# Two of four prefetched weight loads requested as 120 and 8 partitions

## The chip, the cores and the metric

The kernel runs on one core of one Trainium2 chip. The metric is the device time of one execution in microseconds; the time before is the median of 3 runs, 1379.53 us (1378.22 to 1382.62).

## The reference, cut to what matters

Two transformer blocks run one after the other over 256 tokens of width 1024. The first ends with a layer of single experts ("PEER"): from the normalized token a query is made with the weights w_pq, 1024 x 2048; scores against two sets of 128 sub-keys pick 16 of 16384 experts for each of 8 heads; each expert is one row of `expert_down` and one of `expert_up`.

```
def block(xb):
    qh = (xb @ w_pq).reshape(T, P_HEADS, 2, P_KEY_DIM)
    s1 = einsum('thd,nd->thn', qh[:, :, 0], sub_keys1)
    s2 = einsum('thd,nd->thn', qh[:, :, 1], sub_keys2)
    ...
    top_s, pos = lax.top_k(cand_s, P_TOPK)
    eidx = jnp.take_along_axis(cand_i, pos, axis=-1)
    g = jax.nn.softmax(top_s, axis=-1)
    u = expert_down[eidx]
    a = gelu(einsum('thkd,td->thk', u, xb))
    return einsum('thk,thkd->td', g * a, expert_up[eidx])
```

So 8 x 16 x 256 = 32768 rows of 2048 floats (down and up side by side, 8 KB) are fetched by index, 268 MB. The second block (gated linear attention, block attention, a feed-forward of 4096, a gate) is dense and follows.

## The kernel before, in words

All dense weights are cut into halves of 128 partitions x 2048 floats, 1 MB each, in the order of `HALVES`. SyncE (SP) requests one half at a time into a ring of three buffers (`ring`). ScalarE copies a half as the high part of a split product (line 1529) and VectorE subtracts to get the low part (line 2107); TensorE then multiplies three combinations of parts (`prod`, its matmuls on line 859). A request into the ring waits until the low part of the half that last held the buffer is made.

The query weights w_pq are eight halves, pq 0,0 to pq 3,1, numbered from `FIRST_PQ`. Four of them, numbers +1, +2, +6 and +7, don't go through the ring: `AHEAD` gives each a buffer of its own (`raw`, which shares memory with the split parts `hl`), so that they can be fetched before the expert rows. `ASKED_FOR` puts their requests after that of number +5, in the order +6, +7, +1, +2. Each waits on TensorE (line 757) until a half that used the memory has been multiplied (`LEFT`). Each has its semaphore, and ScalarE's split of the half waits for it (`ld`). Number +1 is split first, right after the half `FIRST_PQ`; numbers +2 to +7 are split between the expert rows, one per head.

The expert rows are 256 indirect gathers issued by GpSimd (line 823): gather i fetches one row of 8 KB for each of 128 tokens, 1 MB, into one of `NG` = 8 buffers `rows`. Gather i waits until TensorE is done with gather i - 8, and the first ones also for the indices. Gathers 0 to 7 and 8 to 15 need the first head's indices for the first 128 tokens, gather 16 those for the other 128. For each pair of gathers VectorE makes the dot products with the token (line 2615), ScalarE the gelu (line 1797) and a diagonal matrix of the coefficients (line 1804), and TensorE adds the rows, weighted by it, into PSUM (line 1242). The next load on SP, the first half of `gv` (lines 761 to 763), waits for gather 254.

Of the kernel before, what the change touches and what calls it, by code (L numbers as in the profile page):

```python
# [27 lines left out]
FIRST = {}  # L28
# [38 lines left out]
def program(nc, A, out):  # L67
    ctx = ExitStack()
    with ctx:
# [3 lines left out]
        def count(name, keys, by=1):  # L73
            return Count(ctx.enter_context(nc.semaphore(name)), keys, by)
# [148 lines left out]
        LAST_XO, FIRST_PQ = NUM["xo", 1, 1], NUM["pq", 0, 0]  # L223
# [23 lines left out]
        def loaded(n):  # L247

            if HALVES[n][0] == "ple":
                return PWB[:, :]  # L250
            if n in AHEAD:
                return AHEAD[n][:, :]
            return ring[:, RINGED.index(n) % RING, :]
# [22 lines left out]
        ld = {}  # L276
        for i in range(RING):
            ld.update(count(f"ring{i}", RINGED[i::RING], 16))
        ld[NUM["ple", 0, 0]] = at["wple"]
        for n in AHEAD:  # L280
            ld.update(count(f"ahead{n}", [n], 16))

        GV = NUM["gv", 0, 0]
        gv_first = landed("gv_first")
# [367 lines left out]
        n = NUM["xo", 0, 0]  # L652
# [20 lines left out]
        n = NUM["gv", 0, 0]  # L673
# [52 lines left out]
        for k in range(8):  # L726
            for h in range(2):
                n = NUM["dn", k, h]
# [16 lines left out]
        @block.sync  # L745
        def _(e):
            for tb in range(2):
                e.dma_start(X[:, tb, :], A["x"][tb * 128:tb * 128 + 128, :]).then_inc(at[f"x{tb}"][0], 16)
            for n in ASKED_FOR:
                name, k, h = HALVES[n]  # L750
                if (name, k, h) == ("xv", 0, 0):
                    e.dma_start(PWB[:, :], A["wple"]).then_inc(at["wple"][0], 16)
                    e.dma_start(pT[:, :, :], A["pT"]).then_inc(at["pT"][0], 16)
                if name == "ple":
                    continue
                if n in AHEAD:
                    e.wait_ge(*pe[USED[LEFT[n]]])
                elif RINGED.index(n) >= RING:
                    e.wait_ge(*lo[RINGED[RINGED.index(n) - RING]])
                if n == GV:  # L760
                    e.wait_ge(*gath[254])
                    e.dma_start(loaded(n)[:, 0:1024], A["wt"][FIRST[name] + 2 * k + h][:, 0:1024]).then_inc(gv_first[0], 16)
                    e.dma_start(loaded(n)[:, 1024:2048], A["wt"][FIRST[name] + 2 * k + h][:, 1024:2048]).then_inc(ld[n][0], 16)
                    continue
                e.dma_start(loaded(n), A["wt"][FIRST[name] + 2 * k + h]).then_inc(ld[n][0], 16)
            for k, tb, o, n in LAST:
                c = slice(k * 512 + o, k * 512 + o + n)
                e.wait_ge(*pgo[k, tb, o, n])
                e.dma_start(out[tb * 128:tb * 128 + 128, c], SG[:, tb, c]).then_inc(outs.sem, 16)
            e.wait_ge(*outs[4])  # L770
# [63 lines left out]
        def _(e):  # L834
# [654 lines left out]
            for h in range(2):  # L1489
                n = NUM["pg", 1, h]  # L1490
                e.wait_ge(*lo[n])
                w = [p[:, :].rearrange("p (k n) -> p k n", k=4) for p in PARTS[n]]
                for i, (_, tb, o, c) in enumerate(LAST[2:]):
                    ps = bank(("pg", 1, i)) if h == 0 else ps_of(("pg", 1, i))
                    m = prod(ps[:, 0:c], lambda a, k: XT[a][:, k, tb * 128:tb * 128 + 128],
                             lambda b, k: w[b][:, k % 4, o:o + c], range(4 * h, 4 * h + 4), h == 0, h == 1)
                    if h:
                        mark(m, ("pg", 1, i))
                if h == 0:
                    mark(m, ("used", n))  # L1500
# [585 lines left out]
        def _(e):  # L2086
# [467 lines left out]
            def final_var(tb):  # L2554
                ss, v, r, _, _ = fin[tb]
                e.wait_ge(*sqs["final", tb])
                settle(e.tensor_scalar(v[:, 0:1], ss[:, 0:1], 1.0 / 1024, EPS, ALU.mult, ALU.add))
                settle(e.reciprocal(r[:, 0:1], v[:, 0:1]))
                settle(e.tensor_tensor(v[:, 1:2], ss[:, 1:2], r[:, 0:1], ALU.mult))
                e.tensor_scalar(v[:, 1:2], v[:, 1:2], 1.0 / 1024, EPS, ALU.mult, ALU.add).then_inc(var.sem)  # L2560

            def final_root(tb):
                _, v, r, q, both = fin[tb]
                e.wait_ge(*root["final", tb])
                settle(e.reciprocal(r, r))
                settle(e.tensor_tensor(q, v, r, ALU.mult))
                settle(e.tensor_tensor(q, q, r, ALU.mult))
                settle(e.tensor_scalar(q, q, -0.5, 1.5, ALU.mult, ALU.add))
                e.tensor_tensor(r, r, q, ALU.mult).then_inc(inv.sem)
                e.wait_ge(*inv["final", tb])  # L2570
                settle(e.tensor_tensor(both, r[:, 0:1], r[:, 1:2], ALU.mult))
                for k in range(2):
                    c = slice(512 * k, 512 * k + 512)
                    e.tensor_scalar(HS[tb][:, c], HG[:, tb, c], both, None, ALU.mult).then_inc(dg.sem)
# [370 lines left out]
```

## Time and profile before

| | us |
|---|---|
| median of 3 runs | 1379.53 |
| lowest, highest run | 1378.22, 1382.62 |
| span of the profiled execution | 1378.5 |
| its own time around the span | not on the page |
| TensorE busy | 1250.3 (91%) |
| VectorE busy | 949.2 (69%) |
| ScalarE busy | 587.6 (43%) |
| GpSimd busy | 281.1 (20%) |

The span runs from the first to the last instruction of one profiled execution. Matmuls are pipelined, so a busy TensorE is not TensorE at its peak. In the rows PE is TensorE's matmuls and PEld its weight loads, DVE VectorE, ACT ScalarE, POOL GpSimd, SP SyncE. A DMA share is the mean busy share of the core's 16 DMA engines. The queue q0 (software) carries the gathers, q1 (hardware) what SP requests.

### The profile page before, as it was taken

Reading aid. Unit: us, or ns where it says so; the run is one execution under the profiler, and the core shown is the slowest. Engines: PE = TensorE matmul, PEld = TensorE weight load, DVE = VectorE, ACT = ScalarE, POOL = GpSimd, SP = SyncE. Lnnn points to the kernel's source line nnn. Section 1 sums busy time; section 2 is a strip of 40 time slices with the busy share of each in tenths; the row PEclk is TensorE's granted clock in tenths of the full one; section 3 lists DMA queues with packets and bytes.
Section 4 is the critical chain, followed back from the end, with each engine's and each line's share of the span. In section 5 each row is a group of like instructions: output and inputs, shape, how many; then the busy total and the mean of one; then the engine's idle time right before and its main releaser. Section 6 shows DMA issues by size and latency. Waiting matters only on the chain.

```text
span 1378.5 us, 15321 instructions
## 1 busy us (share of the span) xinstructions
PE 1250.3 (91%) x5496; PEld 860.8 (62%) x5496; DVE 949.2 (69%) x1980; ACT 587.6 (43%) x1046; POOL 281.1 (20%) x281
## 2 busy tenths in 40 slices
PE   9999999888887878888787779799999999999998
PEld 8887898444343434334243224488788888888887
DVE  6766667987777777777777776755756556777445
ACT  5657554333222232322222233474556744654334
POOL 1000002454444444343434344000000000000000
PEclk9999999999999999999999999999999999999999
DMA  7543438999999999999999999744354445455551
GB/s 290 206 169 118 173 124 340 422 421 422 422 421 422 421 422 420 421 418 422 419 421 419 420 413 411 294 154 173 120 192 165 154 162 184 174 184 186 198 196 62
DMA packets 57267, 398.73 MB, mean 289 GB/s; under 512 B 7128, under 2 KB 7640, under 8 KB 9448
## 3 DMA queue, kind: packets, MB, share of 16 engines
q0 software_dynamic: 36864, 268.45, 46.9%
q1 hardware_dynamic: 18288, 126.10, 25.5%
q10 hardware_dynamic: 2040, 3.19, 0.7%
q8 instruction: 45, 0.74, 0.2%
q14 instruction: 30, 0.25, 0.1%
HBM read 396.67 MB, written 1.05 MB: 289 GB/s over the span
## 4 chain that ended last, share of the span: by engine, by line
PE 59%; DMA 29%; DVE 7%; ACT 3%; issue 1%; POOL 0%; SPq 0%; ACTq 0%; DVEq 0%
PE ps L859 37%; DMA B<-in_ex,eidx 29%; PE ps L1242 10%; PE ps L887 4%; DVE B L2615 4%; PE ps L888 2%; ACT diags L1804 1%; ACT hl L1529 1%; DVE hl L2107 1%; ACT av_ L1797 1%; PE ps L1122 1%; PE ps L1104 1%; DMA ring<-in_wt 0%; DVE av_ L2623 0%; PE ps L963 0%
## 5 line engine op out<-in xcount | busy, mean ns | idle before, releaser
L1242 PE MATMUL ps<-B,diags 128*128 128x512 f32 x1024 | 480.9, 614 | 115.1 <-ACT diags L1804 114.9
L1242 PEld LDWEIGHTS ps<-B,diags 128*128 128x128 f32 x1024 | 188.1, 193 | 378.1 <-issue 193.3
L823 POOL DMA_INDIRECT B<-in_ex,eidx x256 | 275.0, 1074 | 581.6 <-PE ps L1242 347.3
L2615 DVE CUSTOM_DVE_ANT_0 B<-B 128x1024 f32<-128x1024 f32 x256 | 310.9, 1222 | 110.9 <-DMA B<-in_ex,eidx 110.6
L2107 DVE TENSOR_TENSOR hl<-ring,hl 128x2048 fp32r<-128x2048 f32 x110 | 251.6, 2290 | 171.0 <-ACT hl L1529 170.8
L1529 ACT ACTIVATE hl<-ring 128x2048 fp32r<-128x2048 f32 x110 | 210.1, 1911 | 131.4 <-PE ps L859 128.5
L859 PE MATMUL ps<-hl,R 128*128 128x512 f32 x912 | 212.1, 391 | 0.3 <-DVE R L2123 0.3
L859 PE MATMUL ps<-hl,XT 128*128 128x512 f32 (+1 forms) x888 | 205.5, 390 | 4.6 <-DVE hl L2107 4.1
L1797 ACT ACTIVATE av_<-av_ 128x2 f32<-128x2 f32 x128 | 26.0, 203 | 411.2 <-DVE av_ L2615 411.1
L859 PEld LDWEIGHTS ps<-hl,R 128*128 128x128 f32 x912 | 169.9, 188 | 36.1 <-DVE R L2123 0.7
L859 PEld LDWEIGHTS ps<-hl,XT 128*128 128x128 f32 x888 | 163.7, 189 | 40.6 <-DVE hl L2107 5.6
L859 PE MATMUL ps<-XT,hl 128*128 128x256 f32 x912 | 126.2, 295 | 0.0
L859 PEld LDWEIGHTS ps<-XT,hl 128*128 128x128 f32 x912 | 113.9, 191 | 13.9 <-issue 13.7
L1804 ACT ACTIVATE diags<-ident,av_ 128x128 f32<-128x128 f32 x256 | 88.8, 394 | 29.4 <-DVE av_ L2623 29.4
L887 PE MATMUL ps<-XT,hl 128*128 128x512 f32 x256 | 90.8, 400 | 0.0
L888 PE MATMUL ps<-XT,hl 128*128 128x256 f32 x256 | 71.9, 281 | 0.0
L887 PEld LDWEIGHTS ps<-XT,hl 128*128 128x128 f32 x256 | 48.1, 188 | 12.4 <-DVE XT L2116 0.3
L888 PEld LDWEIGHTS ps<-XT,hl 128*128 128x128 f32 x256 | 48.4, 189 | 0.0
L2623 DVE TENSOR_TENSOR av_<-av_,gw 128x2 f32<-128x2 f32 x128 | 20.7, 161 | 35.4 <-ACT av_ L1797 35.4
L2060 ACT ACTIVATE B<-ps 128x256 f32<-128x256 f32 x32 | 10.5, 381 | 38.9 <-PE ps L888 38.9
L859 PE MATMUL ps<-R,hl 128*128 128x256 f32 x192 | 24.1, 285 | 0.0
L859 PEld LDWEIGHTS ps<-R,hl 128*128 128x128 f32 x192 | 23.2, 192 | 0.7 <-issue 0.3
(391 smaller groups left out, 1023.0 us busy)
## 6 DMA issues: line engine op xcount, KB each, us to landing
ring<-in_wt SPq DMA_DIRECT2D x112, 1024.0 KB, 4.8
raw<-in_wt SPq DMA_DIRECT2D x4, 1024.0 KB, 5.3
B<-in_ex,eidx POOLq DMA_INDIRECT x256, 13.0
X<-in_x SPq DMA_DIRECT2D x2, 512.0 KB, 4.4
B<-in_mem ACTq DMA_DIRECT2D x1, 1024.0 KB, 9.1
PW<-in_wple SPq DMA_DIRECT2D x1, 1024.0 KB, 7.4
ring<-in_wt SPq DMA_DIRECT2D x2, 512.0 KB, 4.1
out<-B SPq DMA_DIRECT2D x3, 256.0 KB, 2.0
```

The lines of the kernel that those rows point to most:

```text
L823: e.indirect_dma_start(out=rows[i % NG][:, :], out_offset=None, in_=A["ex"], in_offset=bass.IndirectOffsetOnAxis(ap=eidx[:, tb, s:s + 1], ...
L859: m = e.matmul(ps, lhs(a, k), rhs(b, k), start=start and (a, b, k) == (0, 0, ks[0]), stop=stop and (a, b, k) == (1, 0, ks[-1]))
L887: e.matmul(y, w[0][:, i, c * 128:c * 128 + 128], XTT[:, :, i, :], start=i == 0, stop=False)
L888: m = e.matmul(y[:, 0, :], w[1][:, i, c * 128:c * 128 + 128], XT[0][:, i, :], start=False, stop=i == 7)
L1104: m = e.matmul(ps[:, tb * 256:tb * 256 + 256], QT[:, 2 * p + kk, tb * 128:tb * 128 + 128], KT[:, 2 * p + kk, :], start=(kk == 0), stop=(kk ...
L1242: m = e.matmul(acc[tb][hf][:, :], diags[:, i % 4, :], rows[i % NG][:, 1024 + 512 * hf:1536 + 512 * hf], start=(s == 0), stop=(s == 127))
L1529: e.activation(PARTS[i][0][:, :], loaded(i), ACT.Copy).then_inc(hi.sem)
L1797: e.activation(av_[:, tb, s:s + 2], av_[:, tb, s:s + 2], ACT.Gelu).then_inc(gelu.sem)
L1804: e.activation(diags[:, (i + z) % 4, :], ident[:, :], ACT.Copy, scale=av_[:, tb, s + z:s + z + 1]).then_inc(dgx.sem)
L2107: e.tensor_tensor(w[1][:, :], loaded(i), w[0][:, :].bitcast(F32), ALU.subtract).then_inc(lo.sem)
L2615: m = e.tensor_tensor_reduce(R[:, 0:1024], R[:, 0:1024], XG[:, tb, :], 1.0, 0.0, ALU.mult, ALU.add, av_[:, tb, s + z:s + z + 1])
L2623: e.tensor_tensor(av_[:, tb, s:s + 2], av_[:, tb, s:s + 2], gw[:, tb, s:s + 2], ALU.mult).then_inc(coef.sem)
```

## The change

Of the four halves fetched ahead, the last two in the order of requests, numbers +1 and +2, are each requested in two pieces: partitions 0 to 119 and partitions 120 to 127. Each piece adds 16 to the half's semaphore, so the wait of the split is for 32. The memory, the order and the wait ahead of the first piece stay.

```
+        PIECED = (FIRST_PQ + 1, FIRST_PQ + 2)
         for n in AHEAD:
-            ld.update(count(f"ahead{n}", [n], 16))
+            ld.update(count(f"ahead{n}", [n], 32 if n in PIECED else 16))
...
                     e.wait_ge(*lo[RINGED[RINGED.index(n) - RING]])
+                if n in PIECED:
+                    for p in (slice(0, 120), slice(120, 128)):
+                        e.dma_start(loaded(n)[p, :], A["wt"][FIRST[name] + 2 * k + h][p, :]).then_inc(ld[n][0], 16)
+                    continue
                 if n == GV:
```

On SP the requests ahead of the expert rows stood like this. The names raw10, raw11, raw21 and raw01 are the buffers of numbers +6, +7, +1 and +2; what is waited for stands in brackets (pe: TensorE, lo: a split, rows6: gather 254).

```order
L765 DMA ring<-in_wt 128x2048 [waits lo] x20
L765 DMA raw10<-in_wt 128x2048 [waits pe]
L765 DMA raw11<-in_wt 128x2048 [waits pe]
L765 DMA raw21<-in_wt 128x2048 [waits pe]
L765 DMA raw01<-in_wt 128x2048 [waits pe]
L762 DMA ring<-in_wt 128x1024 [waits rows6,lo]
L763 DMA ring<-in_wt 128x1024
```

After the change the same place on SP, with the new line 763 for the pieces, reads:

```order
L770 DMA raw10<-in_wt 128x2048 [waits pe]
L770 DMA raw11<-in_wt 128x2048 [waits pe]
L763 DMA raw21<-in_wt 120x2048 [waits pe]
L763 DMA raw21<-in_wt 8x2048
L763 DMA raw01<-in_wt 120x2048 [waits pe]
L763 DMA raw01<-in_wt 8x2048
L767 DMA ring<-in_wt 128x1024 [waits rows6,lo]
```

Two requests became four; nothing else moved on SP, and on the other engines only line numbers differ.

## Rows read from the trace of the kernel before

**Rows 1.** Three stages: length; busy us (instructions) by engine; clock, DMA share, GB/s.

```profile
0.00:229.00 229.00, 224.99 (x1449) 198.38 (x1450) 150.01 (x310) 129.61 (x219) 7.98 (x26) 1.00 0.53 192
229.00:876.00 647.00, 531.94 (x1511) 250.79 (x1509) 487.10 (x1257) 196.48 (x508) 272.03 (x253) 0.98 1.00 416
876.00:1378.50 502.50, 493.38 (x2540) 411.66 (x2538) 312.11 (x414) 261.47 (x320) 1.08 (x2) 1.00 0.48 170
```

**Rows 2.** The page's chain that ended last, share of the span by engine.

```profile
PE 59%; DMA 29%; DVE 7%; ACT 3%; issue 1%; POOL 0%; SPq 0%; ACTq 0%; DVEq 0%
```

**Rows 3.** The chain in order of time, five pieces: start us, us, what.

```profile
347.76 13.72 DMA B<-in_ex,eidx
...
367.64 13.71 DMA B<-in_ex,eidx
...
841.55 13.70 DMA B<-in_ex,eidx
...
861.40 14.65 DMA B<-in_ex,eidx
...
876.08 1.23 DVE B L2615
```

**Rows 4.** Stretches at the end of the gathers, columns as in rows 1.

```profile
868.00:869.50 1.50, 1.17 (x3) 0.68 (x4) 0.00 (x0) 1.50 (x7) 0.00 (x0) 1.00 0.89 371
...
870.50:871.30 0.80, 0.80 (x3) 0.38 (x2) 0.80 (x2) 0.13 (x1) 0.00 (x0) 1.00 0.08 31
871.30:873.60 2.30, 0.73 (x2) 0.00 (x0) 2.03 (x6) 0.29 (x2) 0.00 (x0) 1.00 0.06 25
```

**Rows 5.** DMA packets between 871.3 and 873.6 us.

```profile
DMA packets 8, 0.06 MB, mean 25 GB/s; under 512 B 1, under 2 KB 1, under 8 KB 1
...
q0 software_dynamic: 8, 0.06, 5.9%
```

**Rows 6.** The tile raw: its requests (ns least/median/most), and landing after issue.

```profile
L765 SPq DMA_DIRECT2D raw<-in_wt x4: 327/328/441, 214.9 to 224.9; - x4
...
DMA to landing us min/median/max: 4.8/5.3/6.9
```

**Rows 7.** SP's own waits: us in total, times, longest.

```profile
SPq L761 <- DMA B<-in_ex,eidx: 648.4, 1, 648.4
```

**Rows 8.** GpSimd's issues by time: start, us, what [idle before <- releaser]; gathers 0, 16.

```profile
225.37 1.11 POOL L823 DMA_INDIRECT B<-in_ex,eidx  x1 [219.28 <-PE ps L859]
...
265.92 1.13 POOL L823 DMA_INDIRECT B<-in_ex,eidx  x1 [5.70 <-PE ps L1242]
```

**Rows 9.** Packets by queue from 226.6 to 228.8, then 228.8 to 229.2 us.

```profile
q1 hardware_dynamic: 103, 0.84, 91.0%
...
q0 software_dynamic: 8, 0.07, 86.2%
q1 hardware_dynamic: 24, 0.09, 55.0%
```

**Rows 10.** Issues at 222.2, 224.9, 225.4, 265.9 us: count, KB, us to landing.

```profile
raw<-in_wt SPq DMA_DIRECT2D x1, 1024.0 KB, 5.5
...
raw<-in_wt SPq DMA_DIRECT2D x1, 1024.0 KB, 5.2
...
B<-in_ex,eidx POOLq DMA_INDIRECT x1, 7.4
...
B<-in_ex,eidx POOLq DMA_INDIRECT x1, 8.0
```

**Rows 11.** ScalarE and VectorE by time: start, us, what [idle before <- releaser].

```profile
227.64 1.91 ACT L1529 ACTIVATE hl<-raw 128x2048 fp32r<-128x2048 f32 x1 [10.92 <-DMA raw<-in_wt]
229.46 2.16 ACT L1749 ACTIVATE XT<-ps,gains 128x128 fp32r<-128x128 f32 x8
...
230.62 2.16 DVE L2368 SCALAR_TENSOR_TENSOR XT<-ps,gains,XT 128x128 fp32r<-128x128 f32 x8 [1.05 <-ACT XT L1749]
...
236.72 1.23 DVE L2615 CUSTOM_DVE_ANT_0 B<-B 128x1024 f32<-128x1024 f32 x1 [1.03 <-DMA B<-in_ex,eidx]
```

## The prediction

> **What bounds the kernel now.** I read the stages first. The span falls into three: up to 229 us TensorE is busy for 225 of 229 us; from 229 to 876 us the DMA engines are busy for the whole of 647 us (share 1.00) while TensorE works 532; after 876 us TensorE is busy again for 493 of 502.5 [rows 1]. The middle stage is the 256 gathers of expert rows. The chain that ended last agrees: 29% of the span lies on the gathers' transfers [rows 2]. The change touches the last two loads ahead of that stage, so what counts is what those loads do to its first and to its last moment.
>
> In the chain by time, two pieces that are eight gathers apart end at 347.76 + 13.72 = 361.48 and 367.64 + 13.71 = 381.35 us [rows 3]: 19.87 us for eight gathers of 1 MB, 2.48 us for one. The last two such pieces end at 855.25 and 876.05, 20.80 us apart; 0.93 us is something else that the DMA engines did in between. The first VectorE instruction on the last gather starts at 876.08, right at the landing.
>
> Then the end of the stage. The DMA share falls from 0.89 (868 to 869.5 us) to 0.08 at 870.5 and to 0.06 between 871.3 and 873.6 [rows 4]. One of sixteen engines is 0.0625; in those 2.3 us eight packets pass, 0.06 MB [rows 5]. So fifteen engines have finished their rows by about 871.3, and one works alone for 876.05 - 871.3 = 4.8 us. I call it the laggard. A gather is complete when its last engine is, so the stage ends when the laggard has moved its 256 shares. A share is 1 MB / 16 = 64 KB, eight rows of 8 KB, and takes 2.48 us, a row 2.48 / 8 = 0.31 us. I see no idle time of it: steps of eight gathers are 19.87 us or more, and the share of all engines stays at 1.00 over the stage. What is taken off its work before the gathers moves the stage's end; what is taken off the others does not.
>
> **The change part by part.** Two requests of 128 rows become two of 120 and two of 8 rows; the number of requests for such halves goes from four to six.
>
> *Issuing.* SP gives out a request in 0.33 to 0.44 us [rows 6], so two more cost SP 0.65 to 0.9 us. Behind them on SP stands the first load after the gathers, which waits 648.4 us for the gathers [rows 7]. That wait hides it: nothing. With the wait gone it would be the 0.9 us. Each pair is counted on its own semaphore to 32, waited for where 16 was; no wait is added to another instruction.
>
> *Dealing the rows.* No row shows how 120 or 8 rows are spread over engines. The nearest rows are those of 128: eight to an engine. If eight stay the share, 120 rows fill fifteen engines and leave one out, and 8 rows are one each for eight engines. Per request then: one engine -8 rows (-2.48 us), eight engines +1 row (+0.31 us), seven unchanged. Over both: -4.97, +0.62 and 0. The other end is 120 rows on eight engines, 15 or 16 rows each with the small piece: +8 rows, +2.48 us per request. I take the first, which keeps the share seen in the rows.
>
> The Trainium skill ("DMA: Bandwidth & Descriptors", "Why a DMA increments its semaphore by 16 and not by 1") says that a request uses the largest number of engines up to 16 that divides its rows, so 15 for 120 and 8 for 8, the lowest-numbered ones. By it the engine left out is the last, and the sum is the first of the two above.
>
> *The laggard is the engine left out.* It does not gain 4.97 us, because there is nothing for it to start on. The first gather is issued at 225.37 us [rows 8] and no gather packet runs before 228.8; by 229.2 eight have begun, beside 24 of the old loads [rows 9]. The old loads are all landed at 224.89 + 5.2 = 230.1 us [rows 6, 10]. An engine without them starts on the gather near 229.0: 1.1 us gained. The lower end is nothing, if packets of both queues alternate as they seem to. The upper end: the descriptors may come sooner to an empty engine, but not before the issue ends, 225.37 + 1.11 = 226.48, so 230.1 - 226.48 = 3.6 us. I take 1.1, by the first gather packets seen.
>
> Part of that is lost again. Gather 16 is issued late, at 265.92, after 5.70 us of waiting [rows 8], and lands 8.0 us later; gather 0, on engines just freed, took 7.4 [rows 10]. So at gather 16 the queues hold only 8.0 - 7.4 = 0.6 us of work in reserve, and an engine that is more than that ahead runs dry. Its issue hangs on VectorE's work since the second gather, which VectorE waited 1.03 us for at 236.72 [rows 11]; if the relieved engine is also last there, this work moves forward by up to 1.03 us. So 0.6 us is kept for certain, at most the 1.1: I take 0.8. The stage's end then moves to about 875.2, and everything behind it, paced by TensorE, moves with it.
>
> *The first cut load's landing.* ScalarE waits 10.92 us for it, until 227.64, and splits it; the turned rows for the query product come next at 229.46, VectorE follows at 230.62 [rows 11]. A ninth row adds up to 0.31 us there. VectorE's later wait of 1.03 us before 236.72 hides it: nothing. Were that cover gone, it is 0.31 us.
>
> Sum: -0.8 us. The page gives of the profiled execution only its span, 1378.5 us; what lies around it is not shown. The median of the three runs is 1379.53, 1.0 above. The step lies inside the span, so I carry it to the median: 1379.53 - 0.8 = 1378.7 us.
>
> **The rivals.**
> *A. The laggard is one of the seven unchanged engines* (two requests share the same sixteen engines as one). Then nothing moves: 1379.5. The trace cannot tell which engine it is; seven of sixteen speak for it. The Trainium skill ("DMA: Bandwidth & Descriptors", "Rules for kernel authors") speaks for it too: splitting a transfer by partitions does not pay, since the parts serialize on the same engines.
>
> *B. The laggard is one of the eight with a ninth row.* It is busy from these loads into the gathers, so both extra rows stay on it to the end: +0.62, 1380.1 us. For it: eight of sixteen. Between this and the forecast I choose by the end of the gathers: fifteen engines end within some 2.5 us (868 to 870.5), and one stands apart by 4.8 [rows 4]. That is one engine with a role of its own, which I take to sit at an end of the order rather than in its middle: the last is left out, the first has a ninth row, and a middle place is mostly A. I lean to the last; that is a choice, not a reading. The Trainium skill (same page, "Latency and other measured facts") calls engines 7 and 15 usually slower; by it the laggard is left out (15) or gets the ninth row (7). No row here names an engine.
>
> *C. 120 rows go to eight engines.* This is the slower side. Those engines carry 2 x 2.48 = 4.97 us more into the gathers; if the laggard is among them, the end is 4.97 late; if not, those eight merely draw level with it (4.8 against 4.97). 1379.53 + 4.97 = 1384.5 us. It decides once the extra work on an engine passes 4.1 us, thirteen rows. Against it: all rows of the trace show eight to an engine.
>
> *D. The empty engine gets its descriptors at once.* 3.6 us, and the first cut load lands before the late engine's share, worth up to the 0.7 us by which it landed later after its issue than the first load (5.5 against the least, 4.8) [rows 6, 10]: 1379.53 - 4.3 = 1375.2 us. Against it: the reserve of 0.6 us at gather 16.
>
> **How the numbers follow.** A measurement of this kernel can tell about 0.3% from no change, 4.1 us; the runs before spread over 4.4. Chances: the forecast 0.50, A 0.15, B 0.20, C 0.07, D 0.08. Only D is faster by over 0.3% and only C slower; the other 0.85 lie within. For the spread of medians I move 0.02 from the middle to each side: 0.10, 0.81, 0.09. The likeliest time is 1378.7. The range leaves out most of C and D. Its low end is the forecast with all that it could gain, 1.1 + 1.03 = 2.1 us, and the 1.3 us by which the lowest run stood under the median: 1379.5 - 2.1 - 1.3 = 1376.1. Its high end is B with half of the 3.1 us by which the highest run stood over it: 1380.1 + 1.6 = 1381.7.
>
> **What would show it.** Right: six requests on that line; the last gather landing near 875.2 and the stretch with a DMA share of 0.06 shorter by about 0.8 us or more; the first gather's landing under 7.4 us after its issue. A: the same end of the stage, 876. B: the stretch longer by about 0.6. C: the cut loads landing more than 2 us later after their issue than now. D: the first gather landing near 5 us after its issue. If the lone engine at the end is gone, or the stage ends over 2 us earlier, the argument on gather 16 is wrong.

## The result: slower by 0.41%

The changed kernel took 1384.96 us (median of 8 runs, 1383.23 to 1387.89), the kernel before 1380.18 on the same chip (8 runs): ratio 1.0041, 95% interval 1.0031 to 1.0051. That is 4.8 us lost; 0.8 were to be won. The profiled execution of the changed kernel took 1387.41, near the top of its runs, so its trace shows a larger loss (span 1385.7 against 1378.5) than the medians do. In its lines a line number is 5 higher than in the kernel before.

### The profile after

First the rate. These are stretches of the kernel before around the first gathers (columns as in [rows 1]; the last three are TensorE's clock, DMA share, GB/s):

```profile
222.00:232.00 10.00, 9.46 (x60) 8.36 (x59) 8.30 (x34) 4.36 (x10) 5.10 (x6) 1.00 0.87 312
232.00:242.00 10.00, 8.25 (x55) 6.70 (x56) 8.41 (x32) 5.10 (x12) 3.16 (x4) 1.00 1.02 425
242.00:262.00 20.00, 15.58 (x56) 8.48 (x55) 18.47 (x52) 4.32 (x14) 9.67 (x8) 0.99 1.01 424
262.00:272.00 10.00, 10.00 (x29) 4.94 (x28) 9.29 (x19) 6.21 (x11) 3.46 (x3) 0.85 1.01 419
272.00:282.00 10.00, 10.00 (x39) 5.75 (x38) 6.26 (x12) 3.23 (x9) 7.12 (x5) 1.00 1.01 420
282.00:302.00 20.00, 16.06 (x54) 8.15 (x52) 18.33 (x56) 5.77 (x14) 9.41 (x8) 1.00 1.01 422
```

The same stretches of the changed kernel:

```profile
222.00:232.00 10.00, 9.37 (x59) 8.24 (x57) 6.93 (x28) 1.44 (x1) 5.09 (x6) 1.00 0.87 193
232.00:242.00 10.00, 7.19 (x35) 7.22 (x35) 5.82 (x18) 6.85 (x17) 0.88 (x1) 0.65 1.01 333
242.00:262.00 20.00, 18.66 (x67) 11.61 (x66) 15.63 (x48) 3.65 (x12) 8.76 (x8) 0.84 1.01 421
262.00:272.00 10.00, 7.19 (x15) 2.79 (x14) 9.32 (x28) 4.46 (x9) 2.45 (x3) 0.85 1.01 419
272.00:282.00 10.00, 10.00 (x34) 5.28 (x32) 9.43 (x17) 3.60 (x7) 5.97 (x5) 0.98 0.93 338
282.00:302.00 20.00, 18.06 (x66) 9.62 (x64) 15.35 (x48) 7.40 (x19) 10.20 (x9) 1.00 1.01 415
```

Look at the last two columns together. In the first two stretches the DMA share is the same as before (0.87, 1.01) and the rate is not: 119 and 92 GB/s are missing, over 10 us each 2.1 MB. At the 420 GB/s that the stage otherwise moves, that is 5.0 us. In the stretch from 272 us the share falls to 0.93 and the rate by more: queues stand empty for a part of it, and a packet that runs takes 0.32 us on average instead of 0.28 (467 packets in 92.6% of 16 engines' 10 us, before 574 in 101.0%). With the stretch behind it 0.96 MB are missing, 2.3 us. Together 7.3 us. The first VectorE instruction on the last gather starts 883.36 - 876.08 = 7.28 us later than in [rows 3]. So the whole loss of this trace is made in the first 80 us of the gathers, and can be counted in bytes that were not moved.

The packets between 229 and 232.4 us in the changed kernel:

```profile
q1 hardware_dynamic: 82, 0.66, 87.8%
q0 software_dynamic: 9, 0.07, 9.3%
```

82 packets take 87.8% of 16 engines' 3.4 us: 0.58 us each. In [rows 9] 103 take 91.0% of 16 x 2.2 us: 0.31 us. A row of a cut half costs nearly twice as much. The same shows in three shorter stretches, of the kernel before and then of the changed kernel:

```profile
224.00:227.00 3.00, 3.00 (x15) 2.48 (x14) 2.83 (x17) 0.00 (x0) 1.32 (x2) 1.00 0.98 369
227.00:228.80 1.80, 1.80 (x16) 1.72 (x15) 1.53 (x4) 1.16 (x1) 1.50 (x2) 1.00 1.00 419
228.80:232.00 3.20, 2.66 (x24) 2.50 (x23) 2.15 (x7) 3.20 (x10) 2.29 (x4) 1.00 0.97 348
...
224.00:227.00 3.00, 3.00 (x15) 2.46 (x14) 2.83 (x16) 0.00 (x0) 1.31 (x2) 1.00 0.96 248
227.00:228.80 1.80, 1.80 (x16) 1.72 (x15) 1.52 (x4) 0.00 (x0) 1.50 (x2) 1.00 1.04 209
228.80:232.00 3.20, 2.57 (x24) 2.38 (x21) 0.79 (x1) 1.44 (x1) 2.29 (x4) 1.00 0.95 205
```

TensorE's product and gather 6 in the kernel before:

```profile
231.89 5.55 PE L859 MATMUL ps<-XT,R 128*128 128x128 f32 x48 [0.54 <-DVE XT L2368]
...
237.71 1.05 POOL L823 DMA_INDIRECT B<-in_ex,eidx  x1 [4.86 <-PE ps L859]
```

In the changed kernel, ScalarE, VectorE and TensorE by time, answering to [rows 11], and GpSimd's gathers 6 and 16, the latter answering to [rows 8]:

```profile
230.56 1.91 ACT L1534 ACTIVATE hl<-raw 128x2048 fp32r<-128x2048 f32 x1 [13.83 <-DMA raw<-in_wt]
232.38 2.15 ACT L1754 ACTIVATE XT<-ps,gains 128x128 fp32r<-128x128 f32 x8
233.53 2.16 DVE L2373 SCALAR_TENSOR_TENSOR XT<-ps,gains,XT 128x128 fp32r<-128x128 f32 x8 [3.95 <-ACT XT L1754]
234.81 10.37 PE L864 MATMUL ps<-XT,R 128*128 128x128 f32 x48 [3.44 <-DVE XT L2373]
...
245.45 0.94 POOL L828 DMA_INDIRECT B<-in_ex,eidx  x1 [12.57 <-PE ps L864]
...
273.08 1.25 POOL L828 DMA_INDIRECT B<-in_ex,eidx  x1 [5.57 <-PE ps L1247]
```

The first cut half is awaited until 230.56 instead of 227.64. ScalarE works through its list in order, so the turned rows behind the split come 2.9 us later as well, then VectorE's part, then TensorE's product of 48 matmuls. That product needs 10.37 us; in the kernel before it starts at 231.89 and takes 5.55. Gather 6 waits for it, and gather 16, issued at 273.08, is 7.16 us later than in [rows 8]: nearly the whole 7.28. Why the product is long shows in two stretches of the changed kernel:

```profile
231.50:234.80 3.30, 0.00 (x0) 0.02 (x1) 1.27 (x5) 3.30 (x10) 1.08 (x2) 1.00 1.02 246
234.80:248.00 13.20, 13.19 (x52) 11.62 (x53) 10.11 (x34) 5.33 (x12) 2.25 (x2) 0.50 1.01 391
```

TensorE does nothing for 3.3 us, and is then granted 0.50 of its clock, the level of 1.2 GHz, until 248 us. In the kernel before it waits 0.54 us at that place and keeps 2.4 GHz.

At the end of the stage, the last piece of the chain and the first work on it, then two stretches and the gathers' own packets of the second of them:

```profile
868.70 14.63 DMA B<-in_ex,eidx
...
883.36 1.23 DVE B L2620
...
878.00:879.80 1.80, 1.31 (x4) 0.24 (x2) 1.80 (x4) 0.00 (x0) 0.00 (x0) 1.00 0.12 50
879.80:883.30 3.50, 2.06 (x5) 1.06 (x6) 2.86 (x9) 0.90 (x3) 0.00 (x0) 1.00 0.42 125
...
q0 software_dynamic: 11, 0.07, 5.0%
```

5.0% of sixteen engines is 0.8 of one: a single engine still ends the stage, some 3.5 us behind the others (4.8 before, [rows 4, 5]).

### The profile page after: what moved, and what is told of

Same layout as the page of the kernel before. It is cut to its first block, busy times and chain, and to the rows that moved or that the text cites. A ratio compares the mean times of both kernels' runs of the same rounds, so it can differ in the third digit from the quotient of the medians.

```text
span 1385.7 us, 15323 instructions
## 1 busy us (share of the span) xinstructions
PE 1257.6 (91%) x5496; PEld 867.5 (63%) x5496; DVE 948.9 (68%) x1980; ACT 587.4 (42%) x1046; POOL 277.2 (20%) x281
## 4 chain that ended last, share of the span: by engine, by line
PE 60%; DMA 27%; DVE 8%; ACT 3%; issue 1%; POOL 0%; SPq 0%; ACTq 0%; DVEq 0%
PE ps L864 37%; DMA B<-in_ex,eidx 26%; PE ps L1247 11%; PE ps L892 4%; DVE B L2620 4%; PE ps L893 2%; DVE hl L2112 1%; ACT hl L1534 1%; ACT diags L1809 1%; ACT av_ L1802 1%; DMA raw<-in_wt 1%; PE ps L1127 1%; PE ps L1109 0%; DMA ring<-in_wt 0%; DVE av_ L2628 0%
## 5 line engine op out<-in xcount | busy, mean ns | idle before, releaser
L828 POOL DMA_INDIRECT B<-in_ex,eidx x256 | 271.2, 1059 | 592.7 <-PE ps L1247 351.7
```

The source lines that it names most:

```text
L828: e.indirect_dma_start(out=rows[i % NG][:, :], out_offset=None, in_=A["ex"], in_offset=bass.IndirectOffsetOnAxis(ap=eidx[:, tb, s:s + 1], ...
```

## The experiments

Each ran beside the kernel before on the same chip; a time is the median, a ratio is to that kernel, with its 95% interval. The lines come from one profiled execution each. "The cut" is the list of two slices of partitions in the changed kernel, "halves +1 and +2" the two that it cuts.

### What makes a cut half slow

**Two equal pieces.**

```diff
-for p in (slice(0, 120), slice(120, 128)):
+for p in (slice(0, 64), slice(64, 128)):
```

> The same two halves cut at partition 64 (64 + 64), so each of the two requests can use all sixteen engines, four rows each. Theory P (a request that spans only part of the partitions deals its rows in blocks of neighbours, and engines meet at the same part of SBUF, so a row takes 0.6 us instead of 0.31): as slow as the changed kernel, the first cut half lands 7 to 8 us after its issue instead of 5.5, the DMA rate between 224 and 229 us is near 210 to 250 GB/s, the time 1383 to 1388 us. Theory N (what is slow is a request on fewer than sixteen engines): rate 370 to 420 GB/s as before and the time within 1 us of before. Theory R (a second request costs by itself): slow like the changed kernel.

1385.03 us, 1.0039 (1.0024 to 1.0053). From 228.8 to 232 us:

```profile
228.80:232.00 3.20, 2.86 (x26) 2.67 (x24) 1.08 (x1) 1.85 (x2) 2.52 (x3) 1.00 1.02 223
```

The DMA share is whole, so no engine stands idle, and the rate is half: it is not an engine left out that costs. N falls. P and R both expected the time; the next run parts them.

**Two pieces by columns.**

```diff
-for p in (slice(0, 120), slice(120, 128)):
-    e.dma_start(loaded(n)[p, :], A["wt"][...][p, :])
+for p in (slice(0, 1024), slice(1024, 2048)):
+    e.dma_start(loaded(n)[:, p], A["wt"][...][:, p])
```

> The same two halves requested in two pieces of all 128 partitions, 1024 columns each (rows of 4 KB). P and N: as before, within 1 us of 1380, rate 370 GB/s or more between 224 and 229 us, since all partitions and sixteen engines are in each request. R: slow like the changed kernel, 1383 to 1388 us.

1380.3 us, 1.0006 (0.9993 to 1.0018). R falls: a second request by itself costs no time that can be measured. The rate is 325 to 341 GB/s between 224 and 232 us, below the 370 that P and N expected:

```profile
224.00:227.00 3.00, 3.00 (x15) 2.46 (x14) 2.86 (x15) 0.00 (x0) 1.11 (x1) 1.00 0.89 341
```

In this profiled execution the first VectorE instruction on the last gather starts at 878.13 us, 2.05 later than before, and what follows takes 499.9 us instead of 502.4. So a loss at the end of the gathers need not show in the time, and one trace bears on the time only within such differences.

**126 and 2.**

```diff
-for p in (slice(0, 120), slice(120, 128)):
+for p in (slice(0, 126), slice(126, 128)):
```

> The two later halves are cut into 126 and 2 partitions instead of 120 and 8. Theory M (meeting): the rows of a partial request are dealt in blocks of neighbours, one block to an engine, and a row is slow only where two engines write to the same part of SBUF at the same moment; blocks of eight rows keep all engines in step (0.6 us a row with 120), blocks of nine rows on fourteen engines do not. It expects rows of 0.31 to 0.35 us, nine of them in 2.8 to 3.2 us, a rate of 320 to 370 GB/s between 224 and 228.8 us, the first cut half landing at 228.0 to 228.8 us, the second at 231 to 232.5 us, and 1379.5 to 1382.0 us. Theory S (size): whatever has fewer than 128 partitions runs at half the rate. It expects 190 to 215 GB/s, the first cut half at 230.5 us or later, TensorE's product 48 matmuls long in 10 us at a granted clock of 0.5, gather 16 near 273 us and 1384.5 to 1386 us.

1381.45 us, 1.0011 (1.0001 to 1.0021). Two stretches, and TensorE's product:

```profile
224.00:227.00 3.00, 3.00 (x15) 2.48 (x14) 2.86 (x15) 0.00 (x0) 1.11 (x1) 1.00 0.85 333
228.80:232.00 3.20, 2.77 (x25) 2.58 (x23) 1.74 (x4) 3.20 (x9) 2.43 (x3) 1.00 1.01 333
...
232.52 8.61 PE L864 MATMUL ps<-XT,R 128*128 128x128 f32 x48 [0.95 <-DVE XT L2373]
```

333 GB/s against 248 and 205 with 120: six rows more, and most of the rate is back. At a share of 0.85 that is 0.33 us for a row, by the first stretch. A request for fewer than 128 partitions is not slow as such, so S falls. M's forecasts of rate, landing (228.27 us) and time are met; that engines meet where they write is not shown by it. This trace, of the slowest of the ten runs, has a loss of its own: behind an idle time of only 0.95 us, some 2 us into the product, TensorE's clock fell, granted 0.50 from 234.8 to 242 us, and the last gather is worked on 3.36 us later than before.

**112 and 16.**

```diff
-for p in (slice(0, 120), slice(120, 128)):
+for p in (slice(0, 112), slice(112, 128)):
```

> The two later halves are cut into 112 and 16 partitions. Theory M: blocks of seven rows on sixteen engines meet seldom, so the 112 rows go at 310 to 350 GB/s (2.5 to 2.9 us a request); the 16 rows, one to an engine, all lie in four groups of four neighbouring partitions and are slow, up to 1.3 us. The first cut half lands at 228.5 to 229.7 us, and the time is 1380.5 to 1383.5 us. Theory S: 112 rows at half the rate, 210 GB/s, the first cut half at 230.3 to 231 us, 1384.5 to 1386 us.

1385.28 us, 1.0043 (1.0027 to 1.006): M's time missed. The rate is in between, from 224 us on:

```profile
224.00:227.00 3.00, 3.00 (x15) 2.49 (x14) 2.85 (x15) 0.00 (x0) 1.20 (x2) 1.00 1.00 292
227.00:228.80 1.80, 1.80 (x16) 1.68 (x15) 1.51 (x4) 0.00 (x0) 1.50 (x2) 1.00 1.03 241
```

but the half was whole only at 231.97 us, later than with 120, where M had 229.7 at the latest. Its 112 rows had landed 5.7 us after their issue, near 228.0; its 16 rows took 9.3 us (those of the later half 12.0). Why the small requests came so late is not settled; this run fits neither theory.

**The source moved, the partitions kept.**

```diff
-e.dma_start(loaded(n)[p, :], A["wt"][FIRST[name] + 2 * k + h][p, :])
+e.dma_start(loaded(n)[p, :], A["wt9"][PIECED.index(n)][p, 0:2048])   # rows 2304 elements apart
```

> The changed kernel, its two halves cut in 120 and 8, read from a copy of the same weights in DRAM whose rows lie 9 KB apart instead of 8 KB, so that the first rows of two engines' blocks lie 72 KB apart in DRAM instead of 64 KB; the partitions written are the same. Theory M on the side of SBUF (two engines meet where they write): nothing changes, 200 to 255 GB/s between 224 and 232 us, 1384 to 1386 us. Theory D (they meet where they read in DRAM): rows of 0.31 to 0.4 us, 320 to 400 GB/s, the first cut half landing before 228.8 us, 1379.5 to 1382 us.

1385.65 us, 1.0044 (1.0027 to 1.0061), and the rate of the changed kernel:

```profile
228.80:232.00 3.20, 2.50 (x23) 2.31 (x21) 0.72 (x1) 2.06 (x2) 2.29 (x4) 1.00 0.96 218
```

Another spacing in DRAM changes nothing, against D; that speaks for the writing side and does not show it. One spacing was tried; others were not.

The Trainium skill ("SBUF — State Buffer", "Door 1: The DMA port swizzle") states that partitions are reached through 16 ports, in groups of four, and that partitions 0 to 63 reach only eight of them, worth 218 GB/s. The 64-partition cut agrees: 223. An estimate from its table, with 0.31 us for a row that has a port to itself and blocks of neighbouring rows (the blocks are an assumption): fifteen engines that step through blocks of eight rows are on eight ports at any moment, and fourteen on blocks of nine spread over nearly all, which gives the large pieces alone 198 and 370 GB/s; measured, with the small pieces among them, 205 to 248 and 333 to 341. With the small pieces of both halves the same working gives 169 for 120 and 8, 211 for 64 and 64, 251 for 112 and 16, 294 for 126 and 2; measured 205 to 248, 210 to 223, 241 to 292, 333 to 341. It has the order about right and not the sizes. For whole halves it would give 211 as well, and they ran at 348 to 419: they must be dealt in another way, and no run shows how rows are dealt. So M is the account that fits best, not one that is shown.

### Where the time is lost

**One half cut at a time.**

```diff
-PIECED = (FIRST_PQ + 1, FIRST_PQ + 2)
+PIECED = (FIRST_PQ + 2,)        # last_only;  first_only: (FIRST_PQ + 1,)
```

> Only the very last half (number +2) is cut in 120 and 8, number +1 is whole. Theory A (the loss comes from the first cut half landing late: ScalarE waits for it ahead of the turned rows, TensorE stands idle and its clock falls): ScalarE's wait ends at 227.6 as before, no drop of the clock at 235 us; what is left is the late first gathers, second gather some 2.5 to 3 us later, of which VectorE's wait of 1.0 us hides nothing on this side, so gather 16 is issued 1 to 3 us later: 1381 to 1383 us. Theory G (the loss comes from the gathers starting late behind both halves): half of the whole loss, about 1382.4, with no way to tell by the time alone; gather 6, issued 245.4 in the changed kernel and 237.7 before, tells them apart: 237.7 by A.

> Only number +1 is cut in 120 and 8, the last half is whole. Theory A: ScalarE's wait ends near 230.5, TensorE idle for 3.4 us before its product for the second half of the tokens, clock 0.5 for some 10 us after, gather 6 issued near 245, gather 16 near 273, time 1383 to 1388 us, all of the loss. Theory G: half of the loss, about 1382.4, gather 6 near 240.

The last alone 1382.77, 1.0017 (1.0008 to 1.0027); the first alone 1386.47, 1.0047 (1.003 to 1.0064). Gather 6 was issued at 237.64 and at 245.83 us, as A expected in both runs; G falls. The first carries as much as both, though it has half of the slow rows. Its trace shows where the rest goes; two stretches of it:

```profile
242.00:262.00 20.00, 18.65 (x69) 11.89 (x68) 14.27 (x41) 2.89 (x10) 9.27 (x8) 0.85 0.92 371
...
272.00:282.00 10.00, 10.00 (x34) 5.14 (x32) 9.43 (x17) 3.60 (x7) 6.12 (x5) 1.00 0.86 309
```

Set against the kernel before, 2.3 us are lost by rate up to 242 us ((312 - 223 + 425 - 419) x 10 / 420), then 2.5 and 2.6 us by empty queues. With both halves cut the slow rows last longer, and the first of these gaps is filled (421 GB/s there). By these traces that is why the two losses do not add.

**TensorE kept busy.**

```diff
-keep_warm(9)
+keep_warm(22)     # matmuls on constants, read by nobody
```

> The changed kernel with 13 more matmuls on constants (their result is read by nobody) ahead of the product that waits for the turned rows, so that TensorE is not idle from 231.5 to 234.8 us. Theory C (clock): the loss of 7.2 us at gather 16 is the late start (2.9 us) plus the granted clock of 0.50 behind the idle time, which makes the product 10.37 us long instead of 5.55. It expects a granted clock near 1.00 from 234.8 us, the product at 5.5 to 5.7 us, gather 6 at 240 to 241.5 us instead of 245.45, gather 16 at 269.5 to 271.8 us (held then by gathers 0 and 1, which land at 238.7 and 241.2 us), and 1381.5 to 1383.8 us. Theory L (landing alone): the gathers that start late set the time, whatever TensorE's clock; the product gets shorter and the time stays at 1384.5 to 1385.5 us.

1385.75 us, 1.0049 (1.0032 to 1.0066): no gain, against C and a little above L's range. Yet C's mechanism is there: the product, VectorE's wait for gather 1, and the matmuls on the first gathered rows:

```profile
235.00 5.55 PE L864 MATMUL ps<-XT,R 128*128 128x128 f32 x48 [0.26 <-DVE XT L2373]
...
241.33 1.22 DVE L2620 CUSTOM_DVE_ANT_0 B<-B 128x1024 f32<-128x1024 f32 x1 [1.14 <-DMA B<-in_ex,eidx]
...
243.79 2.87 PE L1247 MATMUL ps<-B,diags 128*128 128x512 f32 x3 [3.24 <-ACT diags L1809]
```

At the full clock the product is done at 240.6, and the next matmuls wait until 243.79 for gathers 0 and 1, which stand in the queues behind the slow rows. In the changed kernel they start at 244.97. The late product and the late gathers end within 1.2 us of each other; taking one away leaves the other. In this trace the last gather is worked on 6.17 us later than before (7.28 in the changed kernel); the times do not show that gain.

**ScalarE's order changed.**

```diff
-split_to(FIRST_PQ + 1)
 turned(1, 0)
 turned(1, 1)
 square_block(1)
 sqrt(("h2", 1))
+split_to(FIRST_PQ + 1)
```

> The changed kernel, cut in 120 and 8 as it is, with ScalarE's work on the first cut half put behind its work on the turned rows, so that the rows do not wait for the half's landing. Theory A (the loss comes in by ScalarE's order): the turned rows are out at 230.0 to 230.7 us, TensorE's product starts at 231.8 to 232.2 us and takes 5.5 us, gather 6 is issued at 237.5 to 238.5 us; what is left is the loss of the later half as in the kernel with that half alone cut, or a little more, since both halves and gathers 0 and 1 still land late: gather 16 at 269.5 to 271.5 us, 1382.3 to 1384.0 us. Theory L (the late gathers alone): no gain, 1384.5 to 1385.5 us.

1385.56 us, 1.0048 (1.0031 to 1.0065). The same three places:

```profile
231.75 5.55 PE L864 MATMUL ps<-XT,R 128*128 128x128 f32 x48
...
241.87 1.23 DVE L2620 CUSTOM_DVE_ANT_0 B<-B 128x1024 f32<-128x1024 f32 x1 [0.99 <-DMA B<-in_ex,eidx]
...
244.33 2.05 PE L1247 MATMUL ps<-B,diags 128*128 128x512 f32 x2 [7.03 <-ACT diags L1809]
```

The product is where it was before the change, gather 6 is issued at 237.57 as A had it, and no time is won, as L had it. The slow rows alone are enough, through the gathers queued behind them.

**The first half cut, TensorE kept busy.**

```diff
-PIECED = (FIRST_PQ + 1, FIRST_PQ + 2)
+PIECED = (FIRST_PQ + 1,)
-keep_warm(9)
+keep_warm(22)
```

> Only the first of the two halves cut into 120 and 8, and 13 more matmuls on constants ahead of TensorE's product. Theory B (bytes): with the first half alone cut the DMA engines lost 2.3 us by the rate (222 to 242 us) and 5 us by empty queues (242 to 252 and 272 to 282 us); the matmuls keep the clock, the product is done 5 us earlier, gather 6 is issued at 240.5 to 241.5 us and gather 16 at 268.5 to 270 us, so that most of the empty time goes: 1382.0 to 1384.0 us against 1386.47 us without them. Theory L (landing alone): the time stays at 1385.5 to 1387 us.

1382.53 us, 1.0015 (1.0006 to 1.0025), 3.9 us under the same cut without the matmuls (on another chip; its ratio was 1.0047). Its two stretches, to be set against those of the first half alone:

```profile
242.00:262.00 20.00, 17.79 (x60) 9.49 (x60) 18.47 (x55) 3.78 (x13) 9.79 (x9) 1.00 1.01 422
...
272.00:282.00 10.00, 10.00 (x33) 5.18 (x32) 8.90 (x16) 3.13 (x10) 6.77 (x5) 1.00 1.01 415
```

The empty queues are gone, as B expected, and what is left is the rate of one half. Here the gathers are not held by a second slow half, so the late product and its clock decide.

**No cut at all, ScalarE made slow.** Twice, in the kernel before, with 21 and with 35 pieces:

```diff
-e.activation(PARTS[i][0][:, :], loaded(i), ACT.Copy).then_inc(hi.sem)
+for c in range(0, 2048, 100 if i == FIRST_PQ + 1 else 2048):   # 60 in the second run
+    d = min(2048, c + 100 if i == FIRST_PQ + 1 else 2048)
+    m = e.activation(PARTS[i][0][:, c:d], loaded(i)[:, c:d], ACT.Copy)
+m.then_inc(hi.sem)
```

> The kernel before, its requests whole, but ScalarE's rounding of the first of the two halves done in 21 pieces of 100 columns instead of one of 2048, which makes it some 2.9 us longer (0.15 us for each piece more, from 1.91 us for 2048 columns and 0.26 us for 128). Nothing else is changed. Theory B (bytes): the stage of gathers is bound by what the DMA engines move (420 GB/s), and what is lost is the bytes not moved, whether an engine is slow or its queue is empty; a late product of TensorE makes gathers 6 and 16 late, and the queues run empty until they are issued. It expects the product at 234.5 to 235.2 us at a granted clock of 0.50, gather 6 at 245 to 246 us, gather 16 near 273 us, a DMA share well below 1 between 242 and 252 us and between 272 and 282 us, and 1383.5 to 1387 us, as much as the change lost, with no slow request at all. Theory R (rate alone): only the requests' rate counts; 1379.5 to 1381 us.

1383.67 us, 1.0023 (1.0012 to 1.0034): slower, but the delay came out at 1.9 us instead of 2.9, and in the profiled execution the half had landed 0.86 us earlier, at 226.78, so that the product is only 0.98 us late. The runs fell in two groups, three at 1380.9 to 1381.2 and five at 1383.4 to 1384.6; the profiled one is of the lower, and its product ran at the full clock:

```profile
232.87 5.55 PE L859 MATMUL ps<-XT,R 128*128 128x128 f32 x48 [1.63 <-DVE XT L2371]
```

> As the run with 21 pieces, but 35 pieces of 60 columns. Those 21 took 3.77 us, 0.093 us more for each piece than 1.91 us, so 35 take 5.1 us, 3.2 us more than one: as late as the cut half made ScalarE. The requests stay whole. Theory B (bytes): the product starts at 234.0 to 235.0 us behind an idle TensorE, at a granted clock near 0.50 and some 10 us long; gather 6 at 244.5 to 245.5 us, gather 16 at 272 to 273.5 us; the queues run empty, a mean rate clearly under 420 GB/s between 242 and 252 us and between 272 and 282 us (together 1.0 to 2.5 MB not moved), with 377 to 419 GB/s before 229 us as in the kernel before. 1382.5 to 1387 us, and the two kinds of runs that 21 pieces showed (1381 and 1384 us) become one. Theory R (rate alone): 1379.5 to 1381 us.

1385.94 us, 1.0041 (1.0028 to 1.0055). ScalarE's pieces, the product, gathers 6 and 16, and two stretches:

```profile
227.64 5.06 ACT L1531 ACTIVATE hl<-raw 128x60 fp32r<-128x60 f32 x35 [10.38 <-DMA raw<-in_wt]
...
235.02 10.47 PE L859 MATMUL ps<-XT,R 128*128 128x128 f32 x48 [3.14 <-DVE XT L2371]
...
245.77 1.77 POOL L823 DMA_INDIRECT B<-in_ex,eidx  x1 [12.38 <-PE ps L859]
...
273.24 1.12 POOL L823 DMA_INDIRECT B<-in_ex,eidx  x1 [5.71 <-PE ps L1242]
...
242.00:262.00 20.00, 18.66 (x68) 11.85 (x68) 14.12 (x40) 2.82 (x10) 9.20 (x8) 0.84 0.85 338
...
272.00:282.00 10.00, 10.00 (x34) 5.12 (x32) 9.42 (x17) 3.60 (x7) 5.83 (x5) 0.99 0.89 315
```

No request is cut, the first half lands at 227.64 as before, and the ratio is that of the change. Gathers 6 and 16 are within 0.4 us of the changed kernel's, and the bytes are missing in the queues instead: (424 - 338) x 20 and (420 - 315) x 10 GB/s x us, 2.8 MB, 6.6 us. That matches B, except that the 2.8 MB are above its 2.5 and gather 6 is 0.3 us past its range. The profiled execution is the slowest of the six. The runs still spread (1382.0 to 1387.7); the two groups did not become one.

None of the versions beat the kernel before.

## Why the prediction was wrong

**Issuing: right.** Four requests on the line now, 0.28 to 0.41 us each, and SP's wait behind them is 655.3 us instead of 648.4.

**Dealing the rows: the step that failed.** It counted rows on engines and took each at 0.31 us, the time of a row of 128. No row showed a request of 120, and the bounds it drew (fifteen engines or eight) both kept 0.31. Measured is 0.58: in the trace the cut requests lose 5.0 us of the stage's transfer time instead of moving 0.6 to 5 us between engines. That the cut by partitions does it, and not the number of requests or an engine left out, the runs show; why a row is slow they do not. The rival with 120 rows on eight engines gave 1384.5, close to the measured time, and its sign (the cut loads landing over 2 us later) came true, but its mechanism did not: with eight engines at work the DMA share up to 228.8 us would have been about half, and it was 0.96 and 1.04.

**The first cut load's landing: the second failure.** It allowed 0.31 us and named VectorE's 1.03 us wait as cover. The landing moved by 2.9 us, and gather 0, behind it, landed 13.3 us after its issue instead of 7.4 [rows 10]. The step also followed the delay only to VectorE; two instructions further TensorE stood still for 3.44 us and lost half its clock. The delay run with 35 pieces, without a cut, shows that this path alone costs as much as the change.

**The laggard: not decided.** The lone engine stands 3.5 us behind the others instead of 4.8, so some relief may be there. But gather 16 landed 5.8 us after its issue instead of 8.0 [rows 10]: the queues had run empty, and a lead won before it was gone. The step had said that gather 16 keeps only a small reserve; it had not expected the reserve to fall to nothing. It also read the reserve too small: gather 0's 7.4 us was no time of free engines, since they were on the old loads until after 228.8 us [rows 9]; by the 5.8 us the reserve was about 2.2 us, not 0.6 (an estimate). The traces of the other kernels show a single late engine as well, whether or not an engine was left out.

**The stage's bound: right.** The reading that the gathers' stage ends when the bytes are moved held: in eleven of the thirteen traces the bytes missing between 222 and 302 us, at 420 GB/s, give the lateness of the last gather's first VectorE instruction within 0.5 us. By columns they give 2.7 us for 2.05; for 112 and 16 they give 7.5 for 9.27, and where the rest is lost is open. What follows the stage took 499.9 to 502.4 us in these traces, so a trace's lateness is not yet the loss of its time.

## What to carry over

In a stage that the DMA engines bound, count bytes: a slow request and an empty queue cost the same, and what one takes in advance the other no longer does. Read the DMA share and the GB/s together, since a share of 1.0 stood beside half the rate here. Before a load is cut by partitions, measure one cut; a cut by columns moved the same bytes in the same time within the interval (-0.07% to 0.18%). And follow a late landing past the first engine that waits, to the first idle of TensorE: the clock behind it can cost more than the delay (4.8 us on the product, after a delay of 2.9).

## What was not expected of the hardware

- A row of 8 KB took 0.31 us in requests of 128 partitions and 0.58 in requests of 120; from 228.8 to 232 us 126 and 2 partitions ran at 333 GB/s, 120 and 8 at 205, 64 and 64 at 223. Why is open.
- TensorE stood idle for 3.3 us and was then granted 0.50 for 13.2 us of work, which made 48 matmuls 10.37 us long instead of 5.55. After 1.63 us (the shorter delay) and after 0.54 us it ran the same product at 1.00; with 126 and 2 partitions, after only 0.95 us, 0.50 came some 2 us into the product, which took 8.61 us. So the length of the idle time does not decide alone; what does, and whether it parts the two groups of the shorter delay's runs, is not shown.
